# Identity products put into TensorE's waits, and one wait dropped, in a two-layer hybrid attention and mixture-of-experts kernel

## The chip, the cores and the metric

The kernel runs on one core of a Trainium2 chip. The metric is device microseconds of that core, as the median of several executions. Engines: PE is TensorE's matmul, PEld its weight load, DVE VectorE, ACT ScalarE, POOL GpSimd, SP SyncE, which asks for most transfers.

## The reference, cut to what matters

Two layers run over 512 latent and 256 context tokens of width 1024, all in float32. `adaln_params` makes the modulation vectors by a product with `w_mod`; each layer is then mixers and an expert mixture.

```python
for l in range(DEPTH):
    sh_a, sc_a, gt_a, sh_f, sc_f, gt_f = adaln_params(c, w_mod[l], b_mod[l])
    hl = modulate(xl, g_attn[l], sh_a, sc_a)
    hc = modulate(xc, g_attn[l], csh_a, csc_a)
    out_lat, out_ctx = token_mixers(hl, hc, l, not last, w_in[l], ...)   # softmax heads A, B, C, D
    xl = xl + gt_a * out_lat
    hl = modulate(xl, g_ffn[l], sh_f, sc_f)
    xl = xl + gt_f * expert_choice_ffn(hl, ...)   # 16 experts, top_k tokens each, SwiGLU
```

Context tokens pass through the mixers and the experts in the first layer only. In the second layer they give keys and values alone.

## The kernel before, in words

Every engine has one program, written out by hand in the order in which it runs; waits on semaphores (`wait_ge`) tie them together. TensorE's order is that of the block under `@block.tensor`, and nothing reorders its matmuls: an instruction that waits holds back all that stands behind it.

**Start.** Eight 1 MB pieces of `w_mod` come in one after the other. `mod_mult(n)` multiplies piece n (four products); pieces 4 to 7 follow the first turned token tiles. VectorE then adds the bias (line 1770), `mod_transpose(0)` turns the row, VectorE and ScalarE modulate the turned tokens, and `turned(2)`, which needs a bank that ScalarE empties, leads into the input projection: 30 steps of eight products each, and behind them `scores(0)`.

**Attention.** `attention_plan` gives a list of steps, 16 for each tile of 128 query rows (`TURNS` = 16), tiles in the order context 0, context 1, latent 0 to 3. In step s TensorE issues `scores(s)`; turns the probabilities of step s-2 (into the tensor `psT`), which ScalarE evicts (semaphore `PTa`); multiplies those of step s-3 by the values; and then does side work: `router_bias`, `gates`, pieces of the output projection, and `turn`, which turns the next tile's queries or the last tile's C heads (kind "T") through columns 768 to 1023 of `psT`. Turned probabilities of a context tile need columns 0 to 255 of it, those of a latent tile up to 768. ScalarE evicts a turn in its own step order (semaphore `me`), after that step's exponentials; the next turned probabilities wait for `me`. VectorE takes each score's maximum, ScalarE the exponential (semaphore `P`), and the scores two slots on wait for it. In the second layer there are latent tiles only.

**Router and experts.** After attention VectorE ranks the tokens of each expert in ten rounds of max, index and replace. Two small transposes (`dup`) spread the lists, GpSimd gathers the listed rows by indirect DMA, TensorE turns the gathered rows and starts the experts: 4 quarters of 12 stages, 4 MB of weights each, in a ring of 11 slots (first layer) or 17 (second). The ring's next loads wait for a gather's landing (`s_g`, line 628) and then for stages done. In the first layer late pieces of `w_mod` are multiplied between the router and the gather.

Of the kernel before, what the change touches and what calls it, by code (L numbers as in the profile page):

```python
# [15 lines left out]
P = 128  # L16
# [3 lines left out]
TC, TL = CTX // P, LAT // P  # L20
# [33 lines left out]
TURNS = len(UNIT_SLOTS)  # L54
# [129 lines left out]
MOD_FRONT = 4  # L184
MOD_LATE, MOD_LAST = KD, KD
assert (MOD_FRONT * KD + MOD_LATE + MOD_LAST) == 3 * L * KD
LAST_MOD_AT = {"turn": 13, "columns": 14}
MOD_CHUNKS = [(l, r, k) for l in range(L) for r in range(3) for k in range(KD)]
MOD_AT = {(2 + 3 * g + i // 4, 2 * (i % 4) + 1): KD + g * KD + i for g in range(MOD_FRONT - 1) for i in range(KD)}
# [47 lines left out]
def backbone_program(nc, A, out):  # L237
    ctx = ExitStack()
    with ctx:
        def sb(name, cols, dt=f32, rows=P):  # L240
            return ctx.enter_context(nc.sbuf_tensor(name, [rows, cols], dt))
# [11 lines left out]
        ident = sb("ident", P)  # L253
# [142 lines left out]
        def bank(b, p0=0, n=P, col=0, w=512):  # L396
            t, c = BANKS[b]
            return t[p0:p0 + n, c + col:c + col + w]
# [48 lines left out]
        def late_bank(g):  # L447
            return 7 if g == MOD_FRONT else 3
# [305 lines left out]
        def _(pe):  # L754
            def mm(o, lhsT, rhs, start=True, stop=True):
                return nc.tensor.matmul(o, lhsT, rhs, start=start, stop=stop)  # L756

            def tr(o, in_, n=P):
                return nc.tensor.transpose(o, in_, ident[0:n, 0:n])  # L759

            def features(a, x):

                return view(ar, 0, P, a + x // 2 * 256 + x % 2, (2, P))
# [9 lines left out]
            def mod_mult(n):  # L773

                pe.wait_ge(s_w[n % 8], 16 * (n // 8 + 1))
                k = n % 8
                if k == 0 and n:
                    pe.wait_ge(s_mcol, n // 8)
                for j in range(4):
                    if n < KD:  # L780
                        rhs = ar[:, M_RING + n * SLOT + j * 512:M_RING + n * SLOT + (j + 1) * 512]
                    else:
                        i = (n - KD) % MOD_SLOTS
                        t, a = ((gtb, j * 512), (ar, MS1 + j * QNW), (ar, MS2 + j * 512))[i]
                        rhs = t[:, a:a + 512]
                    last = mm(bank(2, 32 * j, 32), scm[:, k * 32:(k + 1) * 32], rhs, k == 0, k == 7)
                last.then_inc(s_mused, 1)

            def mod_transpose(g, b=2):
                pe.wait_ge(s_mrow, g + 1)  # L790
                for t in range(4):
                    if g % 3:
                        row = view(modrow, 0, P, g * 512 + t // 2 * 256 + t % 2, (2, P))
                    else:
                        row = modrow[:, g * 512 + t * P:g * 512 + (t + 1) * P]
                    last = tr(bank(b, col=t * P, w=P), row)
                last.then_inc(s_mT, 1)
# [17 lines left out]
            for l in range(L):  # L815
# [22 lines left out]
                if l == 0:  # L838
                    for n in range(KD // 2, KD):
                        mod_mult(n)  # L840
                    mod_transpose(0)

                tiles = TILES[l]

                def turn(kind, i, name, values=None):

                    n = turns_through(PLANS[l], (kind, i, name))
                    a = QN + tiles[i] * QNW
                    if kind == "Q" and i == 0:
                        b, col = {"A": 7, "B": 6, "D": 5, "C1": 7}[name], 0  # L850
                        if name == "C1":
                            pe.wait_ge(z["me"], 1)
                    else:
                        b, col = 5, 256
                        pe.wait_ge(z["me"], n - 1)
                        if values is not None:
                            pe.wait_ge(z["PTa"], l * TT * TURNS + values + 1)
                    if kind == "T":
                        pe.wait_ge(z["Cn"], l * TT + i + 1)
                        for c in range(2):  # L860
                            last = tr(bank(b, col=col + c * P, w=P), ar[:, OS + c * P:OS + (c + 1) * P])
                    elif name[0] == "B":
                        heads = {"B": (0, 1, 2, 3), "B0": (0, 1), "B1": (2, 3)}[name]
                        for n, h in enumerate(heads):
                            q = a + QN_AT["B"] + 96 * h
                            last = tr(bank(b, 0, 96, col + n * P, P), ar[:, q:q + 96])
                    else:
                        for c in range(2):
                            q = a + QN_AT[name] + c * P
                            last = tr(bank(b, col=col + c * P, w=P), ar[:, q:q + P])  # L870
                    last.then_inc(z["mj"], 1)
# [60 lines left out]
                for tau in range(NSTEP + 4):  # L932
                    for t in EARLY.get(tau, ()) if l == 0 or tau else ():
                        turned(t)
                    if tau < NSTEP:
                        sec, t = STEPS[tau]
                        _, _, nq, ncol = SECTIONS[sec]
# [23 lines left out]
                    b = tau - 1  # L961
# [11 lines left out]
                    b = tau - 2  # L973
# [15 lines left out]
                    if tau == NSTEP:  # L989
                        pe.wait_ge(z["pact"], int(ACT_DONE[NSTEP - TT - 1]))  # L990
                        pe.wait_ge(z["pdve"], int(DVE_DONE[NSTEP - TT - 1]))
                        pe.wait_ge(z["bsd"], TT)
                        pe.wait_ge(z["bsa"], TT)
                        for name in Q_FIRST[:3]:
                            turn("Q", 0, name)
                        scores(0)
                    if l and tau == 3:
                        pe.wait_ge(s_mrow, 3 * L)
                    if l and tau == LAST_MOD_AT["turn"]:
                        mod_transpose(MOD_FRONT + 1, 5)  # L1000
                    for i in k_jobs(tau - 1):
                        n = K_ORDER.index(i)
# [78 lines left out]

                TAIL = tail_steps(PLANS[l], n_tiles - 1)
                for step, (s, v, pv, turns, pieces, ahead) in enumerate(PLANS[l]):
                    if s:
                        scores(s)
                    if v is not None:
# [16 lines left out]
                    if pv is not None:  # L1103
# [5 lines left out]
                        if u % 2:  # L1109
                            for n, k in enumerate(kt):  # L1110
                                for h in range(2):
                                    a, b = PT[(pv - 1 + h) % 3] + n * P, VV + k * 768 + VCOL[u] + 64 * h
# [17 lines left out]
                    if s in GATE_AT[l]:  # L1130
                        n = GATE_AT[l].index(s)
# [9 lines left out]
                    if step in TAIL:  # L1141
                        n = TAIL[step]
# [37 lines left out]
                affinities(1)  # L1180
                gates(5, "fg", (0, 1, 2, 3))
                late = range(MOD_FRONT * KD, (MOD_FRONT + 1) * KD) if l == 0 else ()
                for n in late[:6]:
                    late_mod(n)
                pe.wait_ge(z["fgev"], 4 * l + 4)
# [8 lines left out]
                    late_mod(n)  # L1194
                for g in (MOD_FRONT,) if l == 0 else ():
                    mod_transpose(g, late_bank(g))

                wc = l == 0
                W = SW[l]
# [498 lines left out]
        def _(dve):  # L1698
# [108 lines left out]
            for l in range(L):  # L1807
# [29 lines left out]
                for tau in range(NSTEP + 4):  # L1837
# [15 lines left out]
                    if l == 0 and tau in MOD_T_AT:  # L1853
                        mod_columns(MOD_T_AT[tau])
                    if l and tau == LAST_MOD_AT["columns"]:
                        mod_columns(MOD_FRONT + 1, 5)
# [513 lines left out]
```

## Time and profile before

| | us |
|---|---|
| median of 3 executions (lowest, highest) | 2136.82 (2134.91, 2136.83) |
| profiled execution: its time | 2138.91 |
| profiled execution: span, first to last instruction | 2137.1 |
| PE busy (share of the span) | 1964.0 (92%) |
| DVE busy | 664.1 (31%) |
| ACT busy | 532.1 (25%) |
| mean granted TensorE clock | 0.978 |

The profiled execution's own time is 1.8 us above its span and 2.1 us above the median. Times of the trace count from the span's start. A granted clock of 1.00 is 2.4 GHz, of 0.50 is 1.2 GHz; TensorE has these two levels, so a mean between them says for what part of a stretch each held. Ends of matmuls are modelled: a group's time holds the tail of its last matmul, which overlaps the next group.

### The profile page before, as it was taken

To read this page: it belongs to the slowest core of one execution; us is meant where nothing else is said; L and a number is where in the kernel's file an instruction comes from. 1 tells how busy PE (TensorE), PEld (TensorE's weight loads), DVE (VectorE), ACT (ScalarE), POOL (GpSimd) and SP (SyncE) were. 2 spreads that over 40 slices of the span, in tenths; PEclk is the share of its full clock that TensorE was granted. 3 is DMA by queue.
4 is the path that set the end of the run, shared out by engine and by line. 5 is a ranking of instruction groups with operands and counts; after the bars stand their busy time and mean duration, and the time that the engine had idled before them with its cause. 6 is when DMAs were issued, how large, how long until landed. Compare 5 with 4: busy or idle time off the path is not lost. (4 is left out here: it accounts for less than half of the span.)

```text
span 2137.1 us, 27257 instructions
## 1 busy us (share of the span) xinstructions
PE 1964.0 (92%) x10872; PEld 927.1 (43%) x10872; DVE 664.1 (31%) x1744; ACT 532.1 (25%) x1224; POOL 161.3 (8%) x157
## 2 busy tenths in 40 slices
PE   6999989999979999999999899989997998888875
PEld 3446455556642332323323556455554333333322
DVE  3322345666650100101001632366665011020203
ACT  3111154555530000100100421165554110000001
POOL 1101010000010010020100101000000000000001
PEclk9999989999989999999999999999999999999999
DMA  9832020000199999999999402030007999999995
GB/s 365 305 137 82 2 78 1 1 2 1 40 354 411 422 364 417 379 390 419 364 414 421 157 20 79 8 91 1 21 24 273 373 426 427 426 426 427 427 427 247
DMA packets 90935, 515.66 MB, mean 241 GB/s; under 512 B 10594, under 2 KB 15628, under 8 KB 36540
## 3 DMA queue, kind: packets, MB, share of 16 engines
q1 hardware_dynamic: 84496, 493.29, 57.1%
q0 software_dynamic: 4416, 15.21, 2.4%
q10 hardware_dynamic: 1900, 5.43, 0.6%
q8 instruction: 88, 1.44, 0.3%
q14 instruction: 35, 0.29, 0.0%
HBM read 498.69 MB, written 15.20 MB: 240 GB/s over the span
## 5 line engine op out<-in xcount | busy, mean ns | idle before, releaser
L756 PE MATMUL psS<-arena 128*64 128x512 f32 (+9 forms) x4552 | 1158.3, 556 | 70.7 <-DMA arena<-in_w_up 20.7
L756 PEld LDWEIGHTS psS<-arena 128*64 128x64 f32 (+4 forms) x4552 | 455.5, 158 | 667.3 <-issue 587.7
L2041 DVE TENSOR_REDUCE mx<-psS 128x1 f32<-128x768 f32 (+2 forms) x200 | 165.5, 827 | 151.9 <-PE psS L756 149.9
L1352 ACT ACTIVATE arena<-psT 128x768 f32<-128x768 f32 (+7 forms) x261 | 150.1, 577 | 243.7 <-PE psT L759 230.2
L1352 ACT ACTIVATE arena<-psS 128x128 f32<-128x128 f32 (+5 forms) x158 | 61.8, 420 | 575.7 <-PE psS L756 530.6
L759 PE MATMUL psT<-ident,arena 128*128 128x128 f32 (+1 forms) x1036 | 172.4, 290 | 35.3 <-ACT arena L1352 9.3
L2225 DVE TENSOR_TENSOR arena<-arena,psS 128x512 f32<-128x512 f32 x32 | 20.6, 684 | 550.5 <-PE psS L756 550.5
L759 PEld LDWEIGHTS psT<-ident,arena 128*128 128x128 f32 (+1 forms) x1036 | 119.9, 144 | 134.3 <-issue 96.3
L756 PE MATMUL psT<-arena 128*32 128x512 f32 x1536 | 174.5, 595 | 0.0
L1352 ACT ACTIVATE arena<-psS,nb 128x768 f32<-128x768 f32 (+2 forms) x200 | 157.9, 792 | 1.4
L756 PE MATMUL psM<-arena 128*128 128x512 f32 x288 | 140.9, 611 | 0.0
L676 POOL TENSOR_TENSOR pw<-pw 128x8 f32<-128x8 f32 x46 | 75.4, 1639 | 619.6 <-DVEq L1713 619.6
L756 PE MATMUL psO<-arena 128*64 128x128 f32 (+1 forms) x1600 | 120.2, 289 | 0.0
L1352 ACT ACTIVATE arena<-psO,modcol,eff 128x128 f32<-128x128 f32 (+1 forms) x63 | 28.3, 505 | 356.0 <-PE psO L759 356.0
L756 PEld LDWEIGHTS psO<-arena 128*64 128x64 f32 (+1 forms) x1600 | 92.2, 140 | 21.8 <-issue 21.5
L2239 DVE SCALAR_TENSOR_TENSOR arena<-psS,LG,arena 128x512 f32<-128x512 f32 x32 | 22.5, 746 | 236.5 <-PE psS L756 232.4
L756 PEld LDWEIGHTS psT<-arena 128*32 128x32 f32 x1536 | 45.1, 109 | 115.9 <-issue 114.3
L756 PEld LDWEIGHTS psM<-arena 128*128 128x128 f32 x288 | 49.3, 192 | 39.5 <-issue 39.5
L1352 ACT ACTIVATE output_high<-arena 128x512 fp32r<-128x512 f32 x22 | 12.9, 623 | 191.1 <-DVE arena L2239 191.1
L756 PE MATMUL psS<-arena,scm 128*32 128x512 f32 x320 | 43.2, 636 | 7.5 <-DMA arena<-in_w_mod 6.2
L756 PE MATMUL psS<-X,arena 128*64 128x512 f32 x96 | 43.8, 599 | 3.4 <-DMA arena<-in_w_up 2.5
L756 PE MATMUL psS<-tables,arena 128*64 128x512 f32 x96 | 43.5, 596 | 3.3 <-DMA arena<-in_w_up 2.5
(232 smaller groups left out, 1265.4 us busy)
## 6 DMA issues: line engine op xcount, KB each, us to landing
arena<-in_w_gate SPq DMA_DIRECT2D x117, 1024.0 KB, 14.6
arena<-in_w_up SPq DMA_DIRECT2D x116, 1024.0 KB, 18.7
arena<-in_w_down SPq DMA_DIRECT2D x116, 1024.0 KB, 26.0
arena<-in_w_mod SPq DMA_DIRECT2D x48, 1024.0 KB, 7.5
arena<-in_w_in SPq DMA_DIRECT2D x6, 2048.0 KB, 7.8
arena<-in_w_out SPq DMA_DIRECT2D x8, 512.0 KB, 7.8
arena<-in_w_out SPq DMA_DIRECT2D x2, 2048.0 KB, 15.2
normed_rows<-arena ACTq DMA_DIRECT2D x8, 512.0 KB, 7.3
```

The source lines that it names most:

```text
L676: nc.gpsimd.tensor_tensor(pw[:, 8:16], pw[:, 0:8], pw[:, 16:24], ALU.pow).then_inc(s_pout, 1)
L756: return nc.tensor.matmul(o, lhsT, rhs, start=start, stop=stop)
L759: return nc.tensor.transpose(o, in_, ident[0:n, 0:n])
L1352: return nc.scalar.activation(o, i, f, **kw)
L2041: link(V.reduce_max(mx[:, par:par + 1], view(S, 0, P, 0, (512, 2), (1, n)), axis=AX.XY))
L2225: last = V.tensor_tensor(ar[:, a:a + 512], ar[:, a:a + 512], bank(2 * g + h), ALU.mult)
L2239: last = V.scalar_tensor_tensor(ar[:, a:a + 512], bank(2 * g + h), LG[:, c:c + 1], gate((2 if g == 2 else 0) + h), ALU.mult, ALU.mult)
```

## The change

A helper `keep_busy(n, b)` issues n products of the 128x128 identity with itself into 128 columns of a PSUM bank that nobody reads at the time. It is called after each of `mod_mult(4)` to `mod_mult(7)` (8 products), after `mod_transpose(0)` (14), ahead of `scores(0)` in the first layer (12), ahead of the scores of some steps (table `BUSY_AT`, step: products, for layer one and two), after the gates of the second layer's router (40), and ahead of the gathered rows' transposes (24 in the first layer, 28 in the second). Apart from that, `turn` waits for the eviction of the step's turned probabilities only if those belong to a latent tile. Other engines' programs stay as they were, instruction for instruction.

```diff
+BUSY_AT = ({1: 9, 2: 9, TURNS + 2: 8, 2 * TURNS + 2: 10}, {1: 9, 2: 10, 9: 7, 10: 12})
...
+            def keep_busy(n, b, col=384):
+
+                for _ in range(n):
+                    mm(bank(b, col=col, w=P), ident[:, :], ident[:, :])
...
                     for n in range(KD // 2, KD):
                         mod_mult(n)
+                        keep_busy(8, 3)
                     mod_transpose(0)
+                    keep_busy(14, 3)
...
                         pe.wait_ge(z["me"], n - 1)
-                        if values is not None:
+                        if values is not None and tiles[values // TURNS] >= TC:
                             pe.wait_ge(z["PTa"], l * TT * TURNS + values + 1)
...
                             turn("Q", 0, name)
+                        if l == 0:
+                            keep_busy(12, 2)
                         scores(0)
...
                 for step, (s, v, pv, turns, pieces, ahead) in enumerate(PLANS[l]):
+                    if s in BUSY_AT[l]:
+                        keep_busy(BUSY_AT[l][s], 6)
                     if s:
                         scores(s)
...
                 late = range(MOD_FRONT * KD, (MOD_FRONT + 1) * KD) if l == 0 else ()
+                if l:
+                    keep_busy(40, 6)
...
                     mod_transpose(g, late_bank(g))
+                keep_busy(28 if l else 24, 6)
```

The order of TensorE's instructions at three places, with the semaphores that each waits for. First the head of the first layer's attention before the change: `scores(0)`, the last turned key and query tiles, `scores(1)` and `scores(2)`.

```order
L759 MATMUL psT<-ident,arena 128x128 x2
L756 MATMUL psS<-arena 128x128 [waits me_0,kt_0,qs,pdve_0,pact_0]
L756 MATMUL psS<-arena 128x128
L759 MATMUL psT<-ident,arena 128x128 [waits kt_0,kn_0]
L759 MATMUL psT<-ident,arena 128x128
L759 MATMUL psM<-ident,arena 128x128 [waits me_0]
L759 MATMUL psM<-ident,arena 128x128
L756 MATMUL psS<-arena 128x128 [waits me_0,kt_0]
L756 MATMUL psS<-arena 128x128
L756 MATMUL psS<-arena 128x128 [waits P_0]
```

The same place in the changed kernel (its lines 757 and 760 are lines 756 and 759 of before):

```order
L760 MATMUL psT<-ident,arena 128x128 x2
L757 MATMUL psS<-ident 128x128 x12
L757 MATMUL psS<-arena 128x128 [waits me_0,kt_0,qs,pdve_0,pact_0]
L757 MATMUL psS<-arena 128x128
L760 MATMUL psT<-ident,arena 128x128 [waits kt_0,kn_0]
L760 MATMUL psT<-ident,arena 128x128
L760 MATMUL psM<-ident,arena 128x128 [waits me_0]
L760 MATMUL psM<-ident,arena 128x128
L757 MATMUL psO<-ident 128x128 [waits me_0,kt_0]
L757 MATMUL psO<-ident 128x128 x8
L757 MATMUL psS<-arena 128x128 x2
L757 MATMUL psO<-ident 128x128 x9
```

The twelve products stand ahead of the wait of `scores(0)`. The nine ahead of `scores(1)` stand behind the wait that was its own (`me_0,kt_0`), so they start only when it ends.

Second, step 18 (the second context tile's third), before the change: its scores, turned probabilities, values, the turn of the first tile's C heads (`Cn`), and step 19's scores and turned probabilities.

```order
L756 MATMUL psS<-arena 128x128 [waits P_0,PTa]
L756 MATMUL psS<-arena 128x128
L759 MATMUL psT<-ident,arena 128x128 [waits me_0,PTa,P_0]
L759 MATMUL psT<-ident,arena 128x128
L756 MATMUL psO<-arena 64x128 [waits PTa]
L756 MATMUL psO<-arena 64x128 x3
L756 MATMUL psO<-ident,rr 64x128 [waits rr]
L756 MATMUL psO<-ident,rr 64x128
L759 MATMUL psT<-ident,arena 128x128 [waits Cn,PTa,me_0]
L759 MATMUL psT<-ident,arena 128x128
L756 MATMUL psS<-arena 128x128 [waits P_0]
```

In the changed kernel, from the new products on:

```order
L757 MATMUL psO<-ident 128x128 [waits PTa]
L757 MATMUL psO<-ident 128x128 x7
L757 MATMUL psS<-arena 128x128 [waits P_0]
L757 MATMUL psS<-arena 128x128
L760 MATMUL psT<-ident,arena 128x128 [waits me_0,PTa,P_0]
L760 MATMUL psT<-ident,arena 128x128
L757 MATMUL psO<-arena 64x128 [waits PTa]
L757 MATMUL psO<-arena 64x128 x3
L757 MATMUL psO<-ident,rr 64x128 [waits rr]
L757 MATMUL psO<-ident,rr 64x128
L760 MATMUL psT<-ident,arena 128x128 [waits Cn,me_0]
L760 MATMUL psT<-ident,arena 128x128
```

The products stand ahead of the wait for `P_0`, and the turn's wait has lost `PTa`.

Third, the second layer's ranking in the changed kernel: the gates, the two transposes of the ranked lists (`dup`), and the first gathered rows (`first_rows0`).

```order
L757 MATMUL psS<-modrow,ident 128x512 x4
L757 MATMUL psO<-ident 128x128 x40
L760 MATMUL psT<-ident,arena 128x48 [waits dup,fgev]
L760 MATMUL psT<-ident,arena 128x48 [waits dup]
L757 MATMUL psO<-ident 128x128 x28
L760 MATMUL psS<-ident,arena 128x128 [waits first_rows0]
```

Before, the same rows stand there without the two of products: 40 products are new ahead of the lists' transposes, 28 behind them.

## Rows read from the trace of the kernel before

**Rows 1.** Page, part 2: DMA busy tenths in 40 slices of 53.4 us.

```profile
DMA  9832020000199999999999402030007999999995
```

**Rows 2.** Windows at half clock: stretch, length, busy by engine, PEclk, DMA share, GB/s.

```profile
270.08:280.32 10.24, 10.08 (x54) 8.33 (x52) 3.06 (x12) 3.91 (x17) 0.50 (x2) 0.50 1.02 276
283.73:287.15 3.42, 3.42 (x22) 2.76 (x22) 0.88 (x4) 1.60 (x5) 0.00 (x0) 0.50 0.00 0
311.04:317.87 6.83, 6.52 (x29) 4.29 (x29) 2.17 (x9) 3.25 (x13) 0.00 (x0) 0.50 0.01 2
352.00:358.83 6.83, 6.54 (x28) 3.89 (x27) 3.87 (x11) 4.24 (x13) 0.00 (x0) 0.50 0.00 1
1393.07:1396.48 3.41, 3.41 (x13) 1.78 (x14) 1.54 (x6) 1.99 (x7) 0.00 (x0) 0.50 1.03 215
...
1638.83:1645.65 6.82, 3.41 (x6) 1.56 (x7) 4.75 (x22) 2.10 (x4) 0.38 (x1) 0.50 0.73 236
...
34.56:37.97 3.41, 2.69 (x10) 2.44 (x11) 1.77 (x6) 2.29 (x7) 0.00 (x0) 0.50 1.08 271
...
sum 85.35, PE 67.15 PEld 48.86 DVE 35.87 ACT 28.26 POOL 3.16; mean PE 4.48 PEld 3.26 DVE 2.39 ACT 1.88 POOL 0.21
```

**Rows 3.** Timeline, router bias, eight products: start, us, engine, line, matmul, records.

```profile
273.14 3.43 PE L756 MATMUL psM<-wrt,modcol 128*128 128x16 f32 x16
...
280.95 1.86 PE L756 MATMUL psM<-wrt,modcol 128*128 128x16 f32 x16
```

**Rows 4.** Timeline, PE, start: modulation pieces, row turned, third token tile [idle before].

```profile
24.70 1.92 PE L756 MATMUL psS<-arena,scm 128*32 128x512 f32 x16
...
30.43 1.06 PE L756 MATMUL psS<-arena,scm 128*32 128x512 f32 x8 [1.42 <-DMA arena<-in_w_mod]
32.38 0.66 PE L759 MATMUL psS<-ident,modrow 128*128 128x128 f32 x4 [0.89 <-DVE modrow L1770]
35.28 1.94 PE L759 MATMUL psT<-ident,arena 128*128 128x128 f32 x8 [2.24 <-ACT arena L1352]
```

**Rows 5.** Waits of PE from 44 to 262 us (projection): us, times, longest.

```profile
PE psS L756 <- DMA arena<-in_w_mod: 1.2, 1, 1.2
```

**Rows 6.** Timeline, PE, first layer: scores of step 0 and of steps 1 and 2.

```profile
267.59 0.49 PE L756 MATMUL psS<-arena 64*128 64x128 f32 x4 [1.46 <-DVEq L1934]
...
269.80 1.34 PE L756 MATMUL psS<-arena 64*128 64x128 f32 x8 [1.14 <-ACT arena L1352]
```

**Rows 7.** Waits of PE from 262 to 365 us: for what, us in total, times, longest.

```profile
PE psT L759 <- ACT arena L1352: 2.2, 3, 1.8
```

**Rows 8.** Timeline, step 18: its scores, the turn behind step 18, its eviction.

```profile
307.84 0.49 PE L756 MATMUL psS<-arena 64*128 64x128 f32 x4 [1.02 <-ACT arena L1352]
...
311.35 0.66 PE L759 MATMUL psT<-ident,arena 128*128 128x128 f32 x2 [1.84 <-ACT arena L1352]
...
312.04 0.39 ACT L1352 ACTIVATE arena<-psT 128x256 f32<-128x256 f32 x1
```

**Rows 9.** Timeline, PE, step 34: its scores.

```profile
351.16 0.70 PE L756 MATMUL psS<-arena 64*128 64x256 f32 x4 [1.75 <-ACT arena L1352]
```

**Rows 10.** Timeline, PE, second layer: scores of steps 1, 2 and 10.

```profile
1390.78 0.70 PE L756 MATMUL psS<-arena 64*128 64x256 f32 x4 [1.14 <-ACT arena L1352]
...
1392.96 1.16 PE L756 MATMUL psS<-arena 64*128 64x256 f32 x4 [1.48 <-ACT arena L1352]
...
1419.45 0.93 PE L756 MATMUL psS<-arena 32*128 32x384 f32 x8 [1.80 <-ACT arena L1352]
```

**Rows 11.** Timeline, PE and SP, second layer: gates, list's transpose, next load.

```profile
1642.91 4.96 PE L756 MATMUL psS<-modrow,ident 128*128 128x512 f32 x8
...
1655.16 0.31 PE L759 MATMUL psT<-ident,arena 48*128 48x48 f32 x1 [7.28 <-DVE arena L2169]
...
1663.94 0.43 SPq L523 DMA_DIRECT2D modrow<-in_w_up  x1
```

**Rows 12.** Timeline, PE, first layer's experts: their first wait for weights.

```profile
707.36 3.65 PE L756 MATMUL psS<-arena 128*64 128x512 f32 x16 [1.28 <-DMA arena<-in_w_up]
```

## The prediction

> **What bounds the kernel now.** I read the busy tenths, then the granted clock of every stretch, then TensorE's waits at the places where products are put in. The transfers are busy without a break through both expert stages (slices 12 to 22 and 32 to 39) and idle through most of attention [rows 1]: attention, projection and router run at the pace of a chain through TensorE, VectorE and ScalarE, and the second layer's experts at the pace of their weights. Before the last instructions TensorE was at 1.2 GHz, half its clock, for 85.35 us in 15 stretches, 67.15 us of them busy; the rows shown are those that bear terms below [rows 2]. Each of them follows waits. So the change trades two things: slow work that becomes fast, and products that come too late and hold back what stands behind them.
>
> **Price of a product.** An identity product is two records of 128 columns with 128 columns of weights. The nearest row is the router bias: sixteen records with the same weights took 1.86 us at full clock and 3.43 us at half [rows 3], 0.116 and 0.214 each with the tail of the last. I take 0.22 us a product, 0.43 at half clock. That is longer than the waits to be filled allow nearly everywhere.
>
> **Start.** Pieces 4 and 5 ran together from 24.70, and one piece costs 1.92 - 1.06 = 0.86 us; piece 7 ran at 30.43 [rows 4]. With eight products (1.76 us) behind each, piece 5 runs at 27.3, 6 at 29.9, 7 at 32.6: 2.1 us late. The row's turn came 1.95 us after piece 7 began, so it could come at 34.5, but the last eight products end at 32.6 + 0.86 + 1.76 = 35.2. The third token tile came 2.90 us after that turn (38.1); the fourteen products end at 35.2 + 0.45 + 3.1 = 38.7, against 35.28 before: 3.4 us late. If TensorE stays at full clock, 2.69 us of slow work there [rows 2] takes half, 1.35 back. In the projection that follows TensorE waited once for 1.2 us, for a piece whose transfer hangs on TensorE's own use of an earlier one [rows 5], so hardly anything is swallowed. **+2.0 us**, between +0.8 (that wait swallows its 1.2) and +3.4 (clock as before).
>
> **First layer, first steps.** Ahead of scores 0: twelve products (2.64) in a wait of 1.46, 1.2 late. The turned keys and queries behind come as much later, and scores 1 waited for them until 269.80 [rows 6]; the nine products behind that wait run from about 270.9 to 272.9, scores 1 0.45 us, nine more, and scores 2 start at 275.3 in place of 270.4: 4.9 late. From there to 287.15 TensorE was busy at half clock for 10.08 + 3.42 = 13.5 us [rows 2], which at full clock takes 6.75. That is 1.9 better; but turned probabilities wait for ScalarE to evict the last turn, behind its exponentials, and I let 0.6 go there. **-1.3**, between -3.3 (the first lateness hidden) and +1.5 (half of the saving lost to such waits).
>
> **Turns.** Eleven turns lose a wait. Over the whole stretch turned columns waited for ScalarE three times, 2.2 us, of which 1.84 was one [rows 7]; that one belongs to step 18, below. The rest: **-0.4**, between -0.9 and 0.
>
> **Step 18 and step 34.** At step 18 eight products (1.76) stand in waits of 1.02 and 1.84 [rows 8], so they are free. The turn that ended the 1.84 goes into the wait, but step 19's turned probabilities need its eviction, which ScalarE reaches at 312.04 in either order and ends at 312.43, against the turn itself at 311.35: little is gained by it alone. From 312.43 to 317.87 lie 5.4 us at half clock, 2.7 of which go: **-2.7**, between -0.5 (clock still falls) and -3.3 (all 6.52 halved). At step 34 ten products (2.2) stand in a wait of 1.75 [rows 9]; the turn there keeps its wait (a latent tile), so as at step 18 half of the 3.27 that 6.54 us of slow work could give [rows 2] stays: **-1.6**, between +0.45 and -3.3.
>
> **Second layer, first steps.** Nine products behind the wait of scores 1: 1.98 late. Ten more: scores 2 at 1390.78 + 1.98 + 0.45 + 2.2 = 1395.4 against 1392.96 [rows 10], 2.4 late. What went slowly there, 3.41 us [rows 2], gives 1.7 back on TensorE, but VectorE's maximum and ScalarE's exponential of scores 1 start 2 us later, and the scores two steps on wait for them: **+1.5**, between +0.7 and +2.4. Steps 9 and 10: twelve products (2.64) in a wait of 1.80, and seven before it in a shorter one, against a slow stretch behind: **+0.5**, between 0 and +1.4.
>
> **Ranking.** The gates end 7.28 us before the list's transpose at 1655.16 [rows 11]; forty products take 8.8. The list, the gather and the weights whose loads wait for its landing (1663.94) come 1.5 us later, and from there transfers are the second layer's pace: **+1.4**. Lower bound 0: the gates began at 1642.91 and were at half clock until 1645.65 [rows 2, 11], 2.7 us that full clock would halve. Upper +3.4, if half clock holds through the gates. The 28 products behind, and faster transposes of gathered rows, change TensorE's start only, which the weights hide.
>
> **First gather.** 24 products and quicker transposes move TensorE's start by a microsecond, but it soon waits 1.28 us for weights [rows 12]: **0**, between -1 and +0.5.
>
> **Sum.** 2.0 - 1.3 - 0.4 - 2.7 - 1.6 + 1.5 + 0.5 + 1.4 = -0.6 us. From the profiled execution's 2138.91 that is 2138.3; it stood 2.09 above the median, so 2136.2. About 0.2% (4.3 us) is what a measurement of this kernel can tell from no change: I forecast no change that can be told, its own range 2131 to 2140.
>
> **Rivals.** *Products are cheaper than 0.22.* At 0.16 us they fit the waits: 8 take 1.3, 14 take 2.2, 40 take 6.4 of 7.28. Then the start gives -0.5, the first steps -2.8, the second layer's +1.0, the ranking 0; with -0.4, -2.7 and -1.6 the sum is -7.0, 2129.8. For it: matmul ends are modelled; against it: sixteen records in a row at 0.116. A lateness that is absorbed by VectorE's and ScalarE's chain would give about the same. 0.24. The Trainium skill (TensorE: Matmul & The Clock Gate, Back-to-back issue gap) gives about 81 ns for a matmul of 128 columns in a stream, which at two records a product is an estimate of 0.16 us and this rival's sum; the row has 0.116 a record, and no run here shows the page's.
>
> *Every slow microsecond was on the path.* All 15 stretches go, and the 67.15 busy us halve: -33.6, 2103.2. Against it: the slow clock stands behind waits for ScalarE, VectorE or a gather. 0.02. The Trainium skill (the same page, Terms) takes the penalty as the throttled time by one less the ratio of the clock, which on 85.35 us is an estimate of 42.7 and 2094; that TensorE stood still in a fifth of those stretches speaks against it.
>
> *The clock falls all the same* (slower). If the drops in the first layer's attention come as before, the products are dead weight: 3.4 at the start, 4.9 in the first steps, 0.45 at step 34, 2.0 in the second layer, 1.4 at the ranking, less 0.9: +11.3, 2148.1. It decides from less than half of the saving of 6.75 + 2.7 + 1.6 on, about 5 us lost. For it: the waits for evictions between the products stay as they were. Against it: the products stand just ahead of the stretches that were slow. 0.13.
>
> *The forty products run at half clock* (slower): 17.2 us in 7.28, +9.9 in place of +1.4, 2144.7; slower beyond 0.2% once the list is over 6 us late. Against it: the gates alone brought full clock 2.7 us after they began. 0.06.
>
> **How the numbers follow.** My forecast has 0.55. Its terms' bounds put a fifth of it below -4.3 us and a tenth above +4.3. Faster: 0.11 + 0.24 + 0.02 = 0.37, less 0.01 for the edge of the first rival: 0.36. Slower: 0.05 + 0.13 + 0.06 = 0.24, less 0.02 where the falling clock costs less than 4.3: 0.22. Same 0.42. The range takes in the first rival with a margin of 2 and the small side of the slower ones: 2127.5 to 2143.
>
> **What would show it.** The start is right if the projection begins some 2 us later; the first steps, if step 8's scores follow the projection's end about 1.3 us sooner, at full clock throughout. No low clock behind steps 18 and 34, or those terms are wrong. The list's transpose should come behind the fortieth product, not behind VectorE. A row of products at 0.16 us each, or low clock inside 270 to 290, would make the prediction wrong.

## The result and the profile after

The changed kernel took 2145.58 us (median of six, 2141.07 to 2146.20) beside 2137.11 us of the kernel before (six, 2134.91 to 2140.05): a ratio of 1.0030 (95% interval 1.0020 to 1.0041), slower by 0.3%. A second set of ten executions (run "again") gave 2143.98 beside 2137.81, the same 1.0030. The forecast of 2136.2 (2127.5 to 2143) missed, and its sign with it.

The first rows of its page, part 1 and the granted clock of part 2:

```profile
span 2139.3 us, 28141 instructions
PE 1994.2 (93%) x11320; PEld 967.5 (45%) x11320; DVE 663.4 (31%) x1744; ACT 532.9 (25%) x1224; POOL 161.4 (8%) x157
...
PEclk9999999999999999999999999999999999999998
```

TensorE is busy 30 us longer (1964.0 before), and its mean clock rose from 0.978 to 0.991. What was wanted of the clock came. The timeline of TensorE at the start of the kernel after (start, length, matmul, records; to compare with [rows 4]):

```profile
24.52 1.28 PE L757 MATMUL psS<-arena,scm 128*32 128x512 f32 x8
25.74 2.05 PE L757 MATMUL psS<-ident 128*128 128x128 f32 x16
27.72 1.06 PE L757 MATMUL psS<-arena,scm 128*32 128x512 f32 x8
...
33.68 1.06 PE L757 MATMUL psS<-arena,scm 128*32 128x512 f32 x8
34.67 2.05 PE L757 MATMUL psS<-ident 128*128 128x128 f32 x16
36.56 0.60 PE L760 MATMUL psS<-ident,modrow 128*128 128x128 f32 x4
37.00 3.29 PE L757 MATMUL psS<-ident 128*128 128x128 f32 x28
40.12 1.04 PE L760 MATMUL psT<-ident,arena 128*128 128x128 f32 x8
```

No piece waits for its transfer any more: each stands behind the eight products ahead of it. The row's turn comes at 36.56 in place of 32.38, the third token tile at 40.12 in place of 35.28. Between the groups of 28 records here and of 80 further down (9.09 us) lie 5.80 us for 52 records: 0.112 us a record, 0.223 a product, which was my price.

The first layer's first steps (to compare with [rows 6]):

```profile
268.67 2.84 PE L757 MATMUL psS<-ident 128*128 128x128 f32 x24
271.44 0.49 PE L757 MATMUL psS<-arena 64*128 64x128 f32 x4
...
273.66 2.25 PE L757 MATMUL psO<-ident 128*128 128x128 f32 x18 [1.14 <-ACT arena L1367]
275.83 0.49 PE L757 MATMUL psS<-arena 64*128 64x128 f32 x4
276.25 2.27 PE L757 MATMUL psO<-ident 128*128 128x128 f32 x18
278.46 0.49 PE L757 MATMUL psS<-arena 64*128 64x128 f32 x4
```

Scores 0, 1 and 2 no longer wait themselves. The 1.14 us that scores 1 waited stand ahead of the first nine products, unfilled, and the products come on top. The second layer's first steps show the same (to compare with [rows 10]):

```profile
1388.22 2.25 PE L757 MATMUL psO<-ident 128*128 128x128 f32 x18 [1.14 <-ACT arena L1367]
1390.40 0.70 PE L757 MATMUL psS<-arena 64*128 64x256 f32 x4
1391.03 2.50 PE L757 MATMUL psO<-ident 128*128 128x128 f32 x20
1393.46 0.70 PE L757 MATMUL psS<-arena 64*128 64x256 f32 x4
```

At the second layer's list (to compare with [rows 11]), the first of the two transposes comes right behind the fortieth product, without a wait:

```profile
1643.61 4.97 PE L757 MATMUL psS<-modrow,ident 128*128 128x512 f32 x8
1648.41 9.09 PE L757 MATMUL psO<-ident 128*128 128x128 f32 x80
1657.43 0.26 PE L760 MATMUL psT<-ident,arena 48*128 48x48 f32 x1
...
1666.31 0.43 SPq L524 DMA_DIRECT2D modrow<-in_w_up  x1
```

Behind steps 18 and 34 the clock stands (windows: stretch, length, busy PE, granted clock, DMA share, GB/s; to compare with [rows 2]), and one stretch at half clock is left in the first steps, after 17.85 us of which TensorE was busy for 16.34:

```profile
287.85:291.26 3.41, 3.41 (x21) 0.50 0.00 0
270.00:287.85 17.85, 16.34 (x142) 1.00 0.84 233
...
311.00:318.00 7.00, 5.48 (x45) 1.00 0.00 0
352.00:359.00 7.00, 5.74 (x42) 1.00 0.00 1
```

**Where the time went.** VectorE and ScalarE run the same instructions in every kernel here, so one and the same VectorE instruction can be looked up in each trace. The table gives how many us each stretch of the program took more (+) or less (-) than in the first trace of before, one row for each profiled execution (the names are those of the experiments below). The stretches end at these times of the first trace of before: start 62, first steps 308, step 18 323, step 34 369; "experts" is 584 to 1313 (first layer), "proj" 1313 to 1373 (second layer's projection), "second" 1373 to 1438 (its first ten steps), "list" 1650 to 1831; the last column is the end. What lies between these stretches differs by 0.2 us at most.

```
                      start  first     18     34 experts  proj second   list    end
before                 0.00   0.00   0.00   0.00   0.00   0.00   0.00   0.00   0.00
before_again           1.55  -2.51  -1.50  -1.57  -0.28   0.00  -0.13   0.02  -4.40
before_third           0.56  -0.92  -0.81  -1.57   0.05   0.00   0.45   0.05  -2.16
before_fourth          1.86  -0.37  -0.81  -1.57   0.16   0.00   0.36  -0.32  -0.77
turn_only              1.54   1.88  -2.43  -1.57  -0.05   0.00   0.03  -0.04  -0.57
turn_again             1.42   2.41  -2.42  -1.57  -0.04   0.00   0.18   0.06   0.05
late_steps_only       -0.17  -0.05  -2.42  -1.57  -0.25  -1.69  -0.01   0.01  -6.15
late_again             0.39  -0.90  -0.81  -1.57   2.89  -1.68  -0.12  -0.03  -1.81
late_steps_old_wait    0.29   3.37  -2.42  -1.56  -0.51  -0.01   0.40  -0.38  -0.79
first_steps_only       1.67   1.21  -2.42  -1.56   1.29  -0.35   0.83   0.05   0.70
second_steps_only      2.01   2.42  -2.42  -1.56  -0.91  -1.69   3.26  -0.28   0.96
ranking_only           0.67   1.91  -2.42  -1.57  -1.23  -1.69   0.89   3.07  -0.37
first_layer_sized     -0.13  -1.12  -1.16  -1.57   1.36   1.18   0.43  -0.29  -1.28
sized                 -0.01  -1.08  -0.80  -1.52   0.31  -0.01   1.25   1.01  -0.93
no_start              -0.17   1.60  -2.42  -1.57   3.35   0.00   4.60   2.59   8.15
no_layer2              1.64   2.00  -2.41  -1.57   0.05  -1.69   0.84  -0.18  -1.31
after                  2.70   0.89  -2.42  -1.56  -2.10  -0.08   3.25   1.47   2.16
again                  2.62   1.04  -2.41  -1.57   1.97  -1.69   3.25   1.54   4.90
```

Its row "after" was the fastest of six executions and is only 2.16 us behind the first trace of before, which stands above the median of its kernel (about a third of its other executions took longer): a pair of profiles understates the difference of the medians, 8.5 us, by 6.

### The profile page after: what moved, and what is told of

It is laid out like the page before. It is cut to its first block and busy times, and to the rows that moved or that the text cites. A ratio compares the mean times of both kernels' runs of the same rounds, so it can differ in the third digit from the quotient of the medians.

```text
span 2139.3 us, 28141 instructions
## 1 busy us (share of the span) xinstructions
PE 1994.2 (93%) x11320; PEld 967.5 (45%) x11320; DVE 663.4 (31%) x1744; ACT 532.9 (25%) x1224; POOL 161.4 (8%) x157
## 5 line engine op out<-in xcount | busy, mean ns | idle before, releaser
L760 PE MATMUL psT<-ident,arena 128*128 128x128 f32 (+1 forms) x1036 | 165.9, 282 | 25.8 <-ACT arena L1367 6.8
```

## The experiments

**The turn edit alone**, run twice.

```diff
-BUSY_AT = ({1: 9, 2: 9, TURNS + 2: 8, 2 * TURNS + 2: 10}, {1: 9, 2: 10, 9: 7, 10: 12})
+BUSY_AT = ({}, {})
...
-                        keep_busy(8, 3)
...
-                    keep_busy(14, 3)
...
-                            keep_busy(12, 2)
...
-                    keep_busy(40, 6)
...
-                keep_busy(28 if l else 24, 6)
```

> The kernel after without any identity product: only the turned columns of context tiles no longer wait for the eviction of turned probabilities. Theory late products (what the changed kernel lost it lost where products ran past the end of the wait that they fill): this part alone is worth my terms for the turns, -0.4 us, and at most the 1.84 us of step 18's wait, so 2135.2 to 2136.7 beside 2137.1 before. Rival, the turns themselves cost time (ScalarE's order or a later clock fall): 2139 or more, a ratio over 1.001.

> The turn edit alone once more, beside the run with products at steps 18 and 34. Theory the turns are enough: a ratio near 0.999, within 0.0006 of that run. Rival, without the products the clock falls behind step 18 in some executions: 0.9995 to 1.0, and a stretch at half clock at about 311 us in this profile.

Measured: 2136.84 us, ratio 0.9993 (0.9984 to 1.0002), and 2136.12, 0.9990 (0.9981 to 0.9999). The turns cost nothing that can be told and are worth 1.5 to 2.1 us by the ratios, with no change still inside the first interval; the two traces don't show where. So the changed kernel's products cost 7.1 us by the medians on one chip ("again" less turn_only), about 8 by the ratios.

**Products taken out of the changed kernel**: those of the start; those of the second layer; and the changed kernel as it is.

```diff
# no_start
-                        keep_busy(8, 3)
...
-                    keep_busy(14, 3)
# no_layer2
+BUSY_AT = ({1: 9, 2: 9, TURNS + 2: 8, 2 * TURNS + 2: 10}, {})
...
-                    keep_busy(40, 6)
...
+                keep_busy(0 if l else 24, 6)
```

> The kernel after without the 8 products behind each of the last four pieces and without the 14 behind the first turned row. Theory late products: the start of the kernel after is 2.7 us behind that of before from 60 us on, and nothing later absorbs it, so this runs in 2145.6 - 2.7 = 2142.9 us. Rival, the start's lateness is swallowed before the end or paid back by full clock in the projection: 2145 to 2146. Rival, products draw clock elsewhere: more than 2.7 us better, because a stretch at half clock later in the kernel goes too.

> The kernel after without the second layer's products in attention (9, 10, 7 and 12) and around the gates and the gather (40 and 28). Theory late products: between the two traces the second layer's first steps lost 3.25 us and the list 1.5, so 2145.6 - 4.7 = 2140.9 us. Rival, the clock: without these products the stretch at half clock behind the second layer's first steps comes back, 1.7 us, and the gates and the transposes behind the list stay at half clock longer, so only 1.5 to 3 us come back, 2142.5 to 2144. Rival, attention of the second layer is off the path since weights set its end: the 1.5 us of the list alone, 2144.1.

> The kernel after once more, unchanged, for the profile of an execution nearer to the median: 2145.6 us within 1. The profiled execution of the kernel after was the fastest of six, 4.5 us below their median, at a granted clock of 0.991 against 0.989 for four of the others. Theory clock: an execution of 2145 us shows 5 to 10 us more at half clock, in a stretch where the chain through TensorE sets the pace, and is late by half of that from there on. Rival, transfers: the clock's stretches are the same and the time is lost in an expert stage, where weights set the pace.

Measured: no_start 2142.72, 1.0019 (1.0009 to 1.0029); no_layer2 2139.81, 1.0006 (0.9997 to 1.0015); again 2143.98, 1.0030 (1.0020 to 1.0041). Against "again" on the same chip the start's products cost 1.3 us by the medians, 2.4 by the ratios (2.7 expected), and the second layer's 4.2 or 5.1 (4.7 expected). The intervals of no_start and "again" overlap, so for the start it is the trace that decides: -0.17 without its products, 2.6 and 2.7 with them. Late products explain both; the second layer alone is more than half of the loss. The profiled execution of no_start was the slowest of its nine.

In the table "after" and "again" agree within 0.2 us in each stretch but two. One is the projection: "again" lacks the stretch at half clock at 1349 us, and half of its 3.41 us is the 1.69 (both were at half clock for 27.3 us in all, so the total doesn't tell them apart). The other is the first layer's experts, 4.1 us apart. There a stretch at half clock fell on the 24 products of the gather. The timeline of after, and then of again:

```profile
629.12 5.52 PE L757 MATMUL psO<-ident 128*128 128x128 f32 x48
...
637.80 4.51 PE L757 MATMUL psS<-arena 128*64 128x512 f32 x20 [0.28 <-ACT arena L1367]
```

```profile
629.54 6.66 PE L757 MATMUL psO<-ident 128*128 128x128 f32 x48
...
639.36 3.23 PE L757 MATMUL psS<-arena 128*64 128x512 f32 x14 [0.28 <-ACT arena L1367]
```

The experts began 1.56 us later; the other 2.5 us arose further on: TensorE waited 5.0 us for weights in place of 3.2, and 0.8 us came between 1200 and 1313 us. My expectation named clock and transfers as rivals; both had a part. The products at the gather are not needed for such a swing: late_steps_only and late_again, one kernel without them, lie 3.1 us apart in the same column. Why weights came later by more than the experts' start did stays open.

**The kernel before, three more profiled executions** (no edit).

> The kernel before once more, unchanged, for a second profile of it. Theory fixed places: TensorE falls to half clock at 270 to 287, 311 and 352 us as in the first profile, for about 27 us up to 370 us, since the waits that stand ahead are the same in each execution. Rival, chance of the execution: one or both of the stretches at 311 and 352 are missing or another one is longer, and VectorE's and ScalarE's instructions are shifted by 1 to 3 us against the first profile from there on.

> The kernel before, a third look at where its clock falls. Theory chance of the execution: the stretches at half clock at 311 and 352 us vary between executions; the one at 352 us, on which my term for step 34 rested, is missing again. Rival, fixed places: both are there as in the first profile.

> The kernel before, a fourth look, with the same two expectations as the third: the stretch at half clock at 352 us missing (chance of the execution) or there (a fixed place).

Measured: single times of 2134.51, 2136.76 and 2138.15 us. Windows of before_again, before_third and before_fourth where the first trace was at half clock behind steps 18 and 34 (stretch, length, busy by engine, granted clock, DMA share, GB/s):

```profile
310.21:313.62 3.41, 3.23 (x10) 1.95 (x11) 1.23 (x5) 2.28 (x10) 0.00 (x0) 0.50 0.00 0
346.00:356.00 10.00, 6.57 (x42) 3.85 (x43) 6.66 (x21) 5.63 (x17) 1.56 (x1) 1.00 0.01 3
```

```profile
312.88:316.29 3.41, 3.41 (x16) 2.31 (x16) 0.81 (x4) 1.59 (x7) 0.00 (x0) 0.50 0.02 5
350.43:353.84 3.41, 3.39 (x22) 2.15 (x18) 2.55 (x8) 2.04 (x6) 0.00 (x0) 0.50 0.00 0
```

```profile
314.63:318.04 3.41, 3.41 (x14) 2.11 (x14) 0.86 (x5) 1.49 (x6) 0.00 (x0) 0.50 0.02 5
352.18:355.59 3.41, 3.41 (x22) 2.15 (x18) 2.58 (x9) 1.92 (x6) 0.00 (x0) 0.50 0.02 5
```

Where the first trace shows 6.83 us twice, the others show 3.41 or nothing. Both expectations miss in part: twice the stretch at 352 is there, but half as long, and all three executions pass step 34 in 1.57 us less than the first, whether it is there or not; step 18 they pass in 0.81 to 1.50 less. At 369 us they stand 4.03, 2.75 and 0.88 ahead of the first trace: that was the slowest of four. The Trainium skill (TensorE: Matmul & The Clock Gate, Part 1: The HAM clock gate) says of the low clock at a kernel's start that the same kernel measures a different number of matmuls in it from run to run; these four executions show such a difference in the middle of the program.

**Products at steps 18 and 34 alone**, with the turn edit (twice), and with the old wait put back.

```diff
# late_steps_only, late_again: like turn_only, but
+BUSY_AT = ({TURNS + 2: 8, 2 * TURNS + 2: 10}, {})
# late_steps_old_wait: and
-                        if values is not None and tiles[values // TURNS] >= TC:
+                        if values is not None:
```

> The kernel after with products at two places alone, the 8 at step 18 and the 10 at step 34 of the first layer, beside the turn edit. In the run with the turn edit alone the clock had not fallen at either place, and both traces had gained there what the kernel after gained (2.4 and 1.6 us). Theory the turns did it: these products are worth nothing, at most 0.6 us lost at step 34 where 2.2 us stand in a wait of 1.75, so 2136.8 to 2137.4, like the turn edit alone (2136.8). Rival, the products keep the clock up in those executions in which it would fall: 2133 to 2135.5.

> The run with products at steps 18 and 34 and the turn edit once more, beside the turn edit alone on the same chip. It had a ratio of 0.9988 (0.9979 to 0.9998) against 0.9993 (0.9984 to 1.0002) of the turn edit alone, in other batches. Theory the turns are enough: both the same within 0.0006, near 0.999. Rival, the products add something: 0.9985 against 0.9995 again.

> The 8 and 10 products at steps 18 and 34 alone, with the old wait of turned columns for the eviction of turned probabilities put back: it parts the turns from the products. Theory the turns did it: the stretch at half clock at 311 us comes as in the kernel before, the wait of 1.84 us at step 18 stands, and the 2.4 us that every run with the turn edit gained there shrink to 1 us or none: a ratio of 0.9995 to 1.0003. Rival, the products hold the clock: no stretch behind step 18, most of the 2.4 us stay, and the ratio is 0.9985 to 0.999 as with the turn edit.

Measured: 2135.00, 0.9988 (0.9979 to 0.9998); again 2137.15, 0.9995 (0.9985 to 1.0005); with the old wait 2136.87, 1.0000 (0.9990 to 1.0010). On one chip late_again and turn_again differ by 0.0005 with turn_again ahead, so the products add nothing that can be told. My theory that the turns alone hold the clock at step 18 falls too: with products and the old wait there was no stretch there and the whole 2.42 us came, while late_again has both edits and still this window:

```profile
312.82:316.23 3.41, 3.41 (x18) 2.48 (x18) 0.81 (x4) 1.56 (x7) 0.00 (x0) 0.50 0.02 5
```

and gained 0.81 as before_third did. Neither edit sets the clock at step 18 in each execution, and the 2.42 us of late_steps_old_wait did not show in its times (ratio 1.0000); in its trace the first steps were 3.37 longer. In the table 2.42 comes with a long first stretch (+0.9 to +3.4, but once -0.05) and 0.80 or 0.81 with a short one (-0.4 to -1.1): time lost to half clock lies mostly in one place or in the other. What decides which stays open.

**Products at one place alone**: the first layer's first steps (12, 9, 9); the second layer's attention; its list (40 and 28). The first has the turn edit beside it, the other two the 8 and 10 products of steps 18 and 34 as well; every other call of `keep_busy` is taken out.

```diff
# first_steps_only
+BUSY_AT = ({1: 9, 2: 9}, {})
# second_steps_only
+BUSY_AT = ({TURNS + 2: 8, 2 * TURNS + 2: 10}, {1: 9, 2: 10, 9: 7, 10: 12})
# ranking_only
+                keep_busy(28 if l else 0, 6)
```

> The kernel after with products in the first layer's first steps alone (12 ahead of scores 0, 9 each ahead of scores 1 and 2), beside the turn edit. Theory late products: they hold scores 1 to 3 back by 5.4 us and give 4.4 back by full clock, against the trace of before; beside the turn edit alone, whose first steps were 1.9 us longer than those of before, they gain 1 us or nothing: 2136 to 2137.2. Rival, my prediction: full clock gives all 6.75 us back, 1.3 us better than before, 3 us better than the turn edit alone, 2133.8. Rival, dead weight: 2 us or more lost, 2139.

> The run with products at steps 18 and 34 (2135.0 us, ratio 0.9988), and with it the second layer's products in attention (9, 10, 7 and 12), nothing else. Theory late products: 3.4 us later from 1440 us on than that run, at weights' pace to the end, so a ratio of 1.0004, about 2138.4. Rival, attention of the second layer is hidden by the weights: 2135 to 2136. Rival, my prediction's +2.0: 2137.0.

> The run with products at steps 18 and 34, and with it the second layer's 40 behind the gates and 28 behind the list, nothing else. Theory late products: forty take 8.9 us where the list is ready 7.3 us after the gates, so the list's transpose, the gather and the loads behind it come 1.5 us later: a ratio of 0.9995, about 2136.5; 2.6 where the gates run at half clock to their end. Rival, a gain: full clock in the transposes behind the list shortens TensorE's start and the weights don't hide it: 2134 or less. Rival, hidden: 2135.0.

Measured: first_steps_only 2138.30, 1.0003 (0.9994 to 1.0012); second_steps_only 2139.87, 1.0016 (1.0004 to 1.0027); ranking_only 2137.25, 1.0005 (0.9993 to 1.0017). In the table the second layer's products cost 3.26 us with the first layer's other products gone, as with them, and nothing behind takes it up. The ratio that I expected, 1.0004, is the lower end of its interval. The list cost 3.07, more than the 1.5 that I expected, 1.1 of it because the gates were at half clock for 5.0 us, until 1644.44, against 2.7 in the first traces of before and after (timeline of ranking_only):

```profile
1639.46 6.08 PE L757 MATMUL psS<-modrow,ident 128*128 128x512 f32 x8
1645.38 9.09 PE L757 MATMUL psO<-ident 128*128 128x128 f32 x80
1654.40 0.26 PE L760 MATMUL psT<-ident,arena 48*128 48x48 f32 x1
```

6.08 us for the gates in place of 4.97. Without products behind them, slow gates are covered by the wait. In no_layer2 they were as slow, the list's transpose came 12.25 us after they began, as in the kernel before (1642.91 to 1655.16 in [rows 11]), and the column "list" has -0.18:

```profile
1641.80 6.04 PE L757 MATMUL psS<-modrow,ident 128*128 128x512 f32 x8
1654.05 0.31 PE L760 MATMUL psT<-ident,arena 48*128 48x48 f32 x1 [6.21 <-DVE arena L2182]
```

With the wait full, it goes to the end. The last 0.4 of the 3.07 us arose behind the list and stay open. The first steps are the place where the runs don't decide: 1.2 us longer than in the first trace of before, but the runs without products there took anything from -2.5 to +3.4.

**Numbers cut to what the waits hold**: at all places, and in the first layer alone.

```diff
# sized
+BUSY_AT = ({TURNS + 2: 4, 2 * TURNS + 2: 7}, {2: 6, 10: 8})
...
+                        keep_busy((0, 5, 5, 3)[n - KD // 2], 3)
...
+                    keep_busy(9, 3)
...
+                            keep_busy(6, 2)
...
+                    keep_busy(32, 6)
# first_layer_sized: the same in the first layer, and
+BUSY_AT = ({TURNS + 2: 4, 2 * TURNS + 2: 7}, {})
...
-                    keep_busy(40, 6)
...
+                keep_busy(0 if l else 24, 6)
```

> The kernel after with each number of products cut to what its wait in the trace of before holds at the measured 0.112 us a record, two records a product: 0, 5, 5 and 3 behind the last four pieces, 9 behind the turned row, 6 ahead of scores 0, none ahead of scores 1, 4 at step 18, 7 at step 34; in the second layer none ahead of scores 1, 6 ahead of scores 2, none at step 9, 8 at step 10, 32 behind the gates; 24 and 28 behind the list as they are. Theory late products: nothing is late, so at least as good as the turn edit alone, and what clock is saved comes on top: 2133 to 2136.5. Rival, few products do not hold the clock: 2136.5 to 2137.5. Rival, a product costs more than its length, since what it delays is on the chain: 2139 or more.

> The first layer of the run with cut numbers (0, 5, 5, 3 and 9 at the start, 6 ahead of scores 0, 4 at step 18, 7 at step 34, 24 in the first gather), without any product in the second layer. Theory late products: the run with cut numbers lost 1.2 us in the second layer's first steps and 1.0 at its list, so this comes out 2.2 us under it, a ratio of 1.0000; and where full clock at the start and in the first steps counts, 1 to 1.5 us under the run with products at steps 18 and 34: 0.998. Rival, even products that fit cost something in each execution but the profiled one: 1.0010, like the run with cut numbers.

Measured: 2139.14, 1.0010 (0.9998 to 1.0022), and 2136.01, 0.9999 (0.9991 to 1.0008). The start came out as expected (0.01 us from the fastest trace of before), and the rest didn't: products that fit at full clock don't fit when the clock has fallen. Six products ahead of scores 2 in sized took 2.93 us with their tail, in a wait of 1.48, and the gates ahead of the 32 took 6.38:

```profile
1388.83 2.93 PE L757 MATMUL psO<-ident 128*128 128x128 f32 x12
1391.69 1.23 PE L757 MATMUL psS<-arena 64*128 64x256 f32 x4
...
1641.04 6.38 PE L757 MATMUL psS<-modrow,ident 128*128 128x512 f32 x8
1647.26 7.31 PE L757 MATMUL psO<-ident 128*128 128x128 f32 x64
```

They account for the 1.01 in the table and for most of the 1.25; two executions of before that were at half clock as long there took 0.45 and 0.36 more than the first. Without the second layer's products the loss is gone, but nothing is gained over the turn edit. No version here beats the kernel before by more than 0.2%; the turn edit alone is the best founded, 0.1%, with no change at the edge of its intervals.

## Why the prediction was wrong, point by point

**The step that failed most** is the saving of clock in the first layer's attention. First steps, turns and steps 18 and 34 stand in my sum at -6.0 us together. In the columns first, 18 and 34 of the table the trace of after is 3.1 us shorter than the first trace of before; but three more executions of the *unchanged* kernel are 5.6, 3.3 and 2.8 shorter there. Against the mean of the four, "after" and "again" gained 0.2 us and nothing, with a microsecond or two open either way. I had taken what one execution lost to the clock for a property of the kernel. The second failed step is smaller: the products in the second layer's attention, +2.0 in my sum, cost 3.25.

**Price of a product:** right inside a long row, 0.223 us. The first rival (0.16) is out. What I missed is a price for each row: until the next matmul started, a short row took close to 0.2 us more than its products (eight 1.98 us, from 25.74 to 27.72; nine 2.17, from 273.66 to 275.83). The Trainium skill (TensorE: Matmul & The Clock Gate, Back-to-back issue gap) has about 81 ns for a matmul of 128 columns in a stream; a record took 112 here, and the measurement decides.

**Start, +2.0:** right in mechanism. 2.7 and 2.6 in the two traces of the changed kernel; four executions of before average 1.0, so 1.7 against those. That the size is near is in part luck. The third token tile came 4.84 us late where I had 3.4, since eight products took 1.98 us in place of 1.76 and a piece 0.99 (33.68 to 34.67) in place of 0.86; and 2.1 of it came back by 62 us, where I had 1.35.

**First layer, first steps, -1.3:** wrong by 2.2 in the profile (+0.89). The lateness was 5.4 us where I had 4.9 (scores 2 at 278.46, less the start's 2.70, against 270.4), by the extra of three rows. Of the 6.75 us that full clock was to return, about 1.7 went into the stretch at 287.85, which I had excluded. TensorE had been busy for 16.34 of the 17.85 us ahead of it, so filled waits did not keep the clock up there. My premise that each slow stretch follows waits was already loose for the kernel before: ahead of the one at 283.73, TensorE was busy for 3.30 of the 3.41 us at full clock. What the clock followed at these places stays open.

**Steps 18 and 34, -2.7 and -1.6:** the sizes came out (-2.42, -1.56) by luck of the pair of traces, and the reasoning failed. The stretches that I priced belonged to the execution that was profiled: other executions of the kernel *before* pass step 34 by 1.57 and step 18 by 0.81 to 1.50 faster, without a product. I then subtracted the 2.09 us by which that execution stood above the median as well. Excess and saving were largely the same microseconds, counted twice; against the mean of four executions of before (-0.78 and -1.18) the two steps are worth 2.0 us, not 4.3.

**Turns, -0.4:** not resolved in the trace by itself; with step 18 included, the edit alone is worth 1.5 to 2.1 us by the ratios (0.9993 and 0.9990).

**Second layer, +1.5 and +0.5:** mis-sized, 3.25 measured in every trace where full clock held. Scores 2 came 3.07 us late (1393.46, set back by the 2.57 by which that trace was early there, is 1396.03 against 1392.96) where I had 2.4: 0.2 us because I had given scores of 256 columns the step of 128 (0.63, from 1390.40 to 1391.03, in place of 0.45), 0.4 by the extra of the two rows (2.18 and 2.43 in place of 1.98 and 2.2). Of the 1.7 us that faster TensorE work behind was to give, 0.7 came: the loss stood at 2.4 after some 15 us, where I had 1.5, and at 3.25 after step 10, where I had 2.0. At half clock it was 4.60 (no_start).

**Ranking, +1.4:** right, 1.47 and 1.54; 2.6 and 3.1 where the gates were at half clock for 5 us or more, near the upper bound of 3.4.

**First gather, 0:** right on average and wrong in its range. The first layer's experts took -2.10 and +1.97 in two executions of the same kernel, against a spread of 0.44 in the four of before. Since late_again and late_steps_only, without these products, lie 3.1 apart (2.89 and -0.25), the swing can't be put down to them alone.

**The rival with the falling clock** named the right side by another way: the clock did not fall (27.3 us at half clock ahead of the last instructions in the trace of after, 85.35 before) and the products that outlasted their waits cost time all the same. 58 us less at half clock bought no time. The Trainium skill (TensorE: Matmul & The Clock Gate, Terms) takes the penalty as the throttled time by one less the ratio of the clock, which is an estimate of 29 us for them; these runs gave nothing of it back. Which of the slow stretches lay on waits was not tested one by one; that of the gates did (no_layer2).

**Adding up:** against the mean of four executions of before, the trace of after has +1.7 at the start, +1.8 in the first steps, -2.0 at steps 18 and 34, +3.1 in the second layer, +1.5 at the list: 6.1, beside medians that lie 6.2 and 8.5 apart. The +1.8 and -2.0 are no better known than the spread in those columns allows. The rest, up to 2.4 us, is within the swing of the first layer's experts (4.1 us between after and again) and is not settled.

## What to carry to other kernels

A product that keeps the clock up is free only where its wait holds it at *half* clock, and only if it stands ahead of the instruction that waits. TensorE's matmuls ran in the program's order in every trace here, so a product behind a wait, or past its end, delayed what stood behind it by the part that outlasted the wait, and a short row cost close to 0.2 us more than its products. Before a slow stretch is priced, compare several executions of the kernel before: what one execution lost to the clock is in part its distance from the median, and can't be saved twice. A total at half clock is no measure of lost time; the start of the same instruction in two traces is.

## What was unexpected of the hardware

The same program, same data, fell to 1.2 GHz at different places in each execution: behind step 18 for 6.83, 3.41, 3.41 and 3.41 us, behind step 34 for 6.83, 0, 3.41 and 3.41, and at 270 to 287 us for 13.66, 6.82, 10.24 and 10.24, in four executions of the kernel before. The times differed with it: the four ends lie 4.4 us apart, and at step 34 it was already 4.0.
